# A hybrid encoder trunk on one core: each token block gets its own root, turn and split at the three norm borders

## The chip, the cores and the metric

One core of one Trainium2 chip. The metric is device time in microseconds of one launch; three runs of the kernel before took 2215.88, 2216.30 and 2216.88 us, median 2216.3.

## What is computed

x is 256 tokens by 2048 features, float32. Four sublayers follow, each `x = x + gate * mixer(norm(x) * gain + shift)`: a pooling mixer, a SwiGLU feed-forward (FFN), a gated linear recurrence (HGRN2), a second FFN. Then a last RMS norm.

```python
def rms_norm(x, gain):
    y = x * lax.rsqrt(jnp.mean(x * x, axis=-1, keepdims=True) + EPS)
    return y * gain

for layer in range(2):
    mod = silu(c) @ w_ada[layer] + b_ada[layer]
    sh_m, sc_m, g_m, sh_f, sc_f, g_f = split(mod, 6)
    h = rms_norm(x, norm_mix_gain[layer]) * (1 + sc_m) + sh_m
    y = pool_mixer(h, ...) if layer == 0 else hgrn2_mixer(h, ...)
    x = x + g_m * y
    h = rms_norm(x, norm_ffn_gain[layer]) * (1 + sc_f) + sh_f
    a, b = split(h @ w_ffn_in[layer], 2)
    x = x + g_f * ((silu(a) * b) @ w_ffn_out[layer])
return rms_norm(x, final_gain)
```

## The kernel before

**Tiling.** Tokens are two blocks of 128 (`TB` = 2), features are chunks of 512 (`CH`), each of four groups of 128. A product writes one chunk of 512 output columns for both token blocks into a PSUM tile `prod`. It runs over steps of 128 input features. To reach float32 accuracy with fp32r operands, each operand is split in a high and a low part, and each step is three matmuls per token block: hi x w_hi, hi x w_lo, lo x w_hi (lines 589 to 591), six per step. Weights come in pairs of steps: SyncE loads `raw`, ScalarE copies it to `w_hi` (line 907), VectorE subtracts to get `w_lo` (line 1232). There are four slots for pairs, so the pairs of the first four steps of the next product (`AHEAD` = 4) are made ready before a product ends, and the pair of step 4 is made after it.

**Who orders the work.** Everything is written out by hand. Each engine has its own program in its own order, with semaphores between them; within an engine's queue nothing passes anything. In a product, each engine calls small functions at given steps (`before(k)`, `after(k)`).

**A border** is the place where a residual x is complete and the next product needs norm(x). There are three: FFN 0 to recurrence (`FFN_OUT` to the first product `C_H`), recurrence's output product to FFN 1 (`C_A1`), and FFN 1 to the last norm. At each one:

1. The last four steps of the last product (`last_steps`, line 551) are done block by block: 12 matmuls of token block 0, then 12 of block 1.
2. VectorE (`update_last`, line 1414) multiplies each block by the gate (line 1427) and adds it to `xs` (line 1435). ScalarE (`square_last`, line 950) squares the last chunk of each block and sums it (line 959).
3. After both blocks, VectorE (`last_root`, line 1343) makes the variance of both and its reciprocal (lines 1346, 1349), and ScalarE the root `rstd` (line 977).
4. VectorE normalises a chunk of both blocks into `tok` (`normalise`, line 1367), TensorE turns it (eight 128x128 transposes, line 660; four fill the PSUM tile `small[0]`, four `small[1]`, each holding two feature groups of both blocks), ScalarE multiplies by the gain and adds the shift (`modulate`, line 989, four activations of 128x256), VectorE casts to `h_hi` (line 1371) and subtracts to `h_lo` (line 1374). All of chunk 0, and the turn of chunk 1, stand ahead of the first matmul of the next product. Chunk 1's modulate and split run beside steps 0 to 3.
5. The next product goes step by step, both token blocks in each. In the recurrence a further chunk is turned ahead of step 4 (k % HG == 0 in `features`); in FFN 1 none is.

After chunk 1's split VectorE makes `w_lo` of step 4. In FFN 1 it first does one "fold" (line 1278), a term of the next modulation vector (`w_ada`), which stands at step 2 in its order.

At the last border there is no turn: after the root of both blocks ScalarE scales block 0's first 1536 columns (line 1221) and block 1's first 512 (line 1222), VectorE the rest (lines 1837, 1842), and SyncE stores four pieces (lines 478 to 484).

Of the kernel before, what the change touches and what calls it, by code (L numbers as in the profile page):

```python
# [40 lines left out]
def build(nc, x, c, norm_mix_gain, norm_ffn_gain, w_ada, b_ada, pool_w, pool_scale, hgrn_w_in,  # L41
# [49 lines left out]
    LAST, BLOCKED = (C_OUT0 + NCH - 1, C_WOUT + NCH - 1, C_OUT1 + NCH - 1), 4  # L91
    FFN_IN = [HALF] * (4 * NA) + [KD] * (2 * (NF - NA))
# [71 lines left out]
    with ctx:  # L164
# [155 lines left out]
        block_modulated = sem("block_modulated")  # L320
        h_first = sem("h_first")
# [44 lines left out]
        def _(sp):  # L366
# [173 lines left out]
        def _(pe):  # L540
# [28 lines left out]

            def segment(chunk, hi, lo, first, n, after=None, before=None, begin=True, end=True):  # L570

                par = chunk % 2
                if begin and chunk >= 2:
                    evacuated(pe, chunk - 2)
                for s in range(n):
                    if chunk in LAST and s == n - BLOCKED:
                        last_steps(chunk, hi, lo, first + s)
                        break
                    if before is not None:
# [104 lines left out]
            def features(k):  # L684
                if k == 0:
                    turn_normalised()
# [60 lines left out]
            def ffn_in(layer):  # L747
                def first_half(s):
                    if s == 0 and layer:
                        turn_normalised()  # L750
                        turn_normalised()
                    wait_block(s)
# [145 lines left out]
        def _(act):  # L898
# [51 lines left out]
            def square_last(at):  # L950
                t.tick("upd")
                t.tick("last")
                for tb in range(TB):
                    if tb:
                        act.wait_ge(x_updated, t.get("upd"))
                    else:
                        act.wait_ge(block_updated, t.get("last"))
                    act.wait_ge(squared, t.get("sq"))
                    act.activation(junk[:, :], xs[:, tb, at * CH:(at + 1) * CH], ACT.Square,
                                   accum_out=ssq[:, tb, at:at + 1]).then_inc(squared, 1)  # L960
                    t.tick("sq")
# [48 lines left out]
            def features(k, gains, shifts, ready):  # L1010
                if k == 0:
                    act.wait_ge(gain_ready, ready)
                    modulate(gains, shifts, 0)
                    modulate(gains, shifts, 1)
                if k % HG == 0 and k // HG >= 2:
                    modulate(gains, shifts, k // HG)
# [53 lines left out]
            def ffn_in(layer):  # L1070
# [9 lines left out]
                def in_a(_):  # L1080
                    g = t.get("step")
                    if g == START[base_a]:
                        act.wait_ge(gain_ready, 7 if layer else 3)
                        act.wait_ge(unit_taken, UNIT[(layer, SH_F, 0) if layer else (0, MIX_F, 0)] + 1)
                        modulate(gain, shifts, 0)
                        if layer:
                            modulate(gain, shifts, 1)
# [33 lines left out]
            def ffn_out(layer):  # L1121
# [9 lines left out]
                sqrt_table()  # L1131
                square_last(NCH - 1)
                root()
# [60 lines left out]
            def first_features(k):  # L1194
                features(k, gain, mod[:, 0, 0:KD], 6)
# [17 lines left out]
            sqrt_table()  # L1213
            square_last(NCH - 1)
            root()

            ffn_in(1)
            ffn_out(1)
            act.wait_ge(x_gained, 2)
            act.wait_ge(rstd_ready, t.get("norm"))  # L1220
            act.activation(xs[:, 0, 0:D - CH], xs[:, 0, 0:D - CH], ACT.Copy, scale=rstd[:, 0:1]).then_inc(y_block, 1)
            act.activation(xs[:, 1, 0:CH], xs[:, 1, 0:CH], ACT.Copy, scale=rstd[:, 1:2]).then_inc(y_block, 1)

        @block.vector
        def _(dve):
# [117 lines left out]
            def last_root():  # L1343
                dve.wait_ge(early_ready, t.get("early"))
                dve.wait_ge(squared, t.get("sq"))
                dve.scalar_tensor_tensor(rstd[:, :], ssq[:, :, NCH - 1], 1.0 / D, early[:, :], ALU.mult, ALU.add).then_inc(var_step, 1)
                t.tick("var")
                dve.wait_ge(var_step, t.get("var"))
                dve.reciprocal(rstd[:, :], rstd[:, :]).then_inc(var_ready, 1)
                t.tick("norm")  # L1350
# [62 lines left out]

            def update_last(chunk_at, at, gates, unit):

                par = chunk_at % 2
# [4 lines left out]
                t.tick("last")  # L1421
                for tb in range(TB):
                    if tb:
                        multiplied(dve, chunk_at)
                    else:
                        dve.wait_ge(block_multiplied, t.get("last"))
                    gated = dve.tensor_tensor(tok[:, tb], prod[par][:, tb], gates, ALU.mult)
                    if tb:
                        gated.then_inc(prod_free[par], 1)
                        evacuated(dve, chunk_at)  # L1430
                    else:
                        gated.then_inc(block_gated, 1)
                        dve.wait_ge(block_gated, t.get("last"))
                    xc = xs[:, tb, at * CH:(at + 1) * CH]
                    added = dve.tensor_tensor(xc, xc, tok[:, tb], ALU.add)
                    if tb:
                        added.then_inc(x_updated, 1)
                    else:
                        added.then_inc(block_updated, 1)
                t.tick("sq", TB)  # L1440

# [123 lines left out]
            def ffn_in(layer):  # L1565
# [33 lines left out]
                def first_half(k):  # L1599
                    if k == 0:  # L1600
                        if layer:
                            normalise(0)
                            normalise(1, 1)
                        split_feat(0)
                        if layer:
                            split_feat(1)
# [50 lines left out]
            def ffn_out(layer):  # L1657
# [16 lines left out]
                last_root()  # L1674
# [156 lines left out]
            last_root()  # L1831
            ffn_in(1)
            ffn_out(1)
            dve.wait_ge(rstd_ready, t.get("norm"))
            for tb in range(TB):
# [27 lines left out]
```

## Time and profile before

| | |
|---|---|
| median of three runs | 2216.3 us |
| profiled execution, first to last instruction (span; no other time of it is recorded) | 2214.7 us |
| TensorE matmul busy | 2161.9 us, 98% of the span |
| VectorE busy | 1659.7 us, 75% |
| ScalarE busy | 998.5 us, 45% |
| mean granted TensorE clock | 0.989 |
| DMA | 574 MB, 259 GB/s |

A matmul's end is modelled, so busy TensorE isn't TensorE at its peak. The time in brackets in a timeline row is how long the engine was idle just before, and which instruction ended that. "Issue" there means that no releaser is seen.

### The profile page before, as it was taken

How to read it: one execution, taken by the hardware profiler on the slowest of the kernel's cores; microseconds unless marked ns; L12 is line 12 of the kernel's file. 1: busy time of each engine (PE TensorE's matmuls, PEld its weight loads, DVE VectorE, ACT ScalarE, POOL GpSimd, SP SyncE). 2: the span in 40 equal slices, each digit the busy share in tenths (PEclk: the TensorE clock that was granted, in tenths of full speed). 3: DMA queues.
4: the chain of work that ended last, by engine and by line, in shares of the span. 5: the costliest groups of instructions: out<-in, count | busy, mean ns of one | idle time of the engine just before them, and what ended most of it. 6: DMA issues, size and time to landing. Idle time of an engine off the chain costs nothing.

```text
span 2214.7 us, 25203 instructions
## 1 busy us (share of the span) xinstructions
PE 2161.9 (98%) x9785; PEld 1753.5 (79%) x9785; DVE 1659.7 (75%) x1709; ACT 998.5 (45%) x1116; POOL 17.9 (1%) x77
## 2 busy tenths in 40 slices
PE   7999999999999999999999999999999999999997
PEld 3547887888888888788888888878888888888886
DVE  5779899999988876578787888677755678456644
ACT  3224544444444444454645455544454444444343
POOL 1000000000000000100000000000000000000000
PEclk9999999999999999999999999999999999999999
DMA  9999998999899987476656664578866687658664
GB/s 374 407 399 350 330 336 305 320 321 317 312 343 312 325 296 239 148 237 202 216 171 206 203 200 136 181 248 301 301 183 190 190 265 258 181 190 290 242 214 138
DMA packets 250356, 574.38 MB, mean 259 GB/s; under 512 B 17558, under 2 KB 17750, under 8 KB 249724
## 3 DMA queue, kind: packets, MB, share of 16 engines
q1 hardware_dynamic: 250236, 572.77, 75.8%
q8 instruction: 77, 1.26, 0.2%
q14 instruction: 43, 0.35, 0.0%
HBM read 570.60 MB, written 2.10 MB: 259 GB/s over the span
## 4 chain that ended last, share of the span: by engine, by line
PE 91%; DVE 3%; SPq 2%; issue 2%; DMA 1%; ACT 1%; ACTq 0%; DVEq 0%
PE prod L589 27%; PE prod L591 27%; PE prod L590 27%; PE small L834 2%; PE modp L617 2%; DVE acc L1281 2%; PE small L660 1%; SPq L399 1%; DMA ada<-in_w_ada 1%; PE modp L651 1%; SPq L374 1%; PE small L806 0%; DMA ada_head<-in_w_ada 0%; PE modp L624 0%; DVE part_value L1577 0%
## 5 line engine op out<-in xcount | busy, mean ns | idle before, releaser
L907 ACT ACTIVATE w_hi<-raw 128x1024 fp32r<-128x1024 f32 x696 | 736.3, 1061 | 1025.4 <-PE prod L591 960.6
L1232 DVE TENSOR_TENSOR w_lo<-raw,w_hi 128x1024 fp32r<-128x1024 f32 x696 | 847.7, 1222 | 431.7 <-ACT w_hi L907 430.3
L589 PE MATMUL prod<-w_hi,h_hi 128*128 128x512 f32 x2072 | 821.4, 396 | 4.9 <-issue 1.9
L591 PE MATMUL prod<-w_hi,h_lo 128*128 128x512 f32 x2072 | 809.4, 391 | 0.0
L590 PE MATMUL prod<-w_lo,h_hi 128*128 128x512 f32 x2072 | 808.8, 390 | 0.0
L589 PEld LDWEIGHTS prod<-w_hi,h_hi 128*128 128x128 f32 x2072 | 390.9, 189 | 87.2 <-issue 3.4
L591 PEld LDWEIGHTS prod<-w_hi,h_lo 128*128 128x128 f32 x2072 | 390.4, 188 | 82.6
L590 PEld LDWEIGHTS prod<-w_lo,h_hi 128*128 128x128 f32 x2072 | 390.9, 189 | 79.7 <-issue 1.4
L1281 DVE SCALAR_TENSOR_TENSOR acc<-ada,cond,acc 128x1024 f32<-128x1024 f32 x255 | 325.8, 1278 | 0.4
L589 PE MATMUL prod<-w_hi,g_hi 128*128 128x512 f32 x688 | 268.8, 391 | 0.0
L591 PE MATMUL prod<-w_hi,g_lo 128*128 128x512 f32 x688 | 267.7, 389 | 0.0
L590 PE MATMUL prod<-w_lo,g_hi 128*128 128x512 f32 x688 | 267.7, 389 | 0.0
L589 PEld LDWEIGHTS prod<-w_hi,g_hi 128*128 128x128 f32 x688 | 129.2, 188 | 27.2 <-issue 0.5
L590 PEld LDWEIGHTS prod<-w_lo,g_hi 128*128 128x128 f32 x688 | 129.2, 188 | 27.1 <-issue 0.5
L591 PEld LDWEIGHTS prod<-w_hi,g_lo 128*128 128x128 f32 x688 | 129.2, 188 | 26.9
L617 PE MATMUL modp<-ada,cond_rows 128*128 128x512 f32 x112 | 58.3, 681 | 13.1 <-DMA brows<-in_b_ada 7.5
L617 PEld LDWEIGHTS modp<-ada,cond_rows 128*128 128x128 f32 x112 | 24.1, 221 | 43.9 <-issue 41.2
L834 PEld LDWEIGHTS small<-qdec,kdec 128*128 128x128 f32 (+1 forms) x448 | 50.6, 184 | 3.3 <-issue 1.4
L834 PE MATMUL small<-qdec,kdec 128*128 128x64 f32 (+1 forms) x448 | 50.0, 265 | 0.0
L660 PE MATMUL small<-ident,tok 128*128 128x128 f32 x272 | 37.8, 285 | 9.8 <-issue 7.9
L660 PEld LDWEIGHTS small<-ident,tok 128*128 128x128 f32 x272 | 33.2, 146 | 15.7 <-issue 9.2
L617 PE MATMUL modp<-ada_head,cond_rows 128*128 128x512 f32 x96 | 42.3, 592 | 0.0
(183 smaller groups left out, 1080.1 us busy)
## 6 DMA issues: line engine op xcount, KB each, us to landing
raw<-in_w_ffn_in SPq DMA_DIRECT2D x352, 512.0 KB, 4.8
ada<-in_w_ada SPq DMA_DIRECT2D x300, 512.0 KB, 6.1
raw<-in_w_ffn_out SPq DMA_DIRECT2D x176, 512.0 KB, 4.6
raw<-in_hgrn_w_in SPq DMA_DIRECT2D x128, 512.0 KB, 3.9
ada_head<-in_w_ada SPq DMA_DIRECT2D x84, 512.0 KB, 14.9
raw<-in_hgrn_w_out SPq DMA_DIRECT2D x32, 512.0 KB, 3.7
raw<-in_pool_w SPq DMA_DIRECT2D x8, 512.0 KB, 15.7
xs<-in_x SPq DMA_DIRECT2D x2, 1024.0 KB, 17.1
```

The source lines that it names most:

```text
L374: sp.dma_start(raw[:, slot], src.rearrange("(a p) n -> p a n", p=P)).then_inc(raw_loaded[slot], 16)
L399: sp.dma_start(ada_buffer(slot), block[:, at:at + UW]).then_inc(ada_loaded[slot], 16)
L589: pe.matmul(o, hi[:, k, ts], wh, start=(begin and s == 0), stop=False)
L590: pe.matmul(o, hi[:, k, ts], wl, start=False, stop=False)
L591: mm = pe.matmul(o, lo[:, k, ts], wh, start=False, stop=(end and s == n - 1))
L617: mm = pe.matmul(modp[:, o], cond_rows[:, k], ada_buffer(slot)[:, o * CH:(o + 1) * CH], start=(k == 0), stop=(in_columns(u) and k == n_row ...
L651: mm = pe.matmul(modp[:, o], ones[:, :], a[:, o * CH:(o + 1) * CH], start=not begun, stop=True)
L660: mm = pe.transpose(small[half][:, o:o + P], block_of(tb, 2 * half + j), ident[:, :])
L834: mm = pe.matmul(small[b][0:keys, o:o + H], kdec[:, b, hd, blk * P:blk * P + keys], qdec[:, b, hd, blk * H:(blk + 1) * H], start=True, sto ...
L907: act.activation(w_hi[:, slot], raw[:, r], ACT.Copy).then_inc(hi_ready, 1)
L1232: dve.tensor_tensor(w_lo[:, slot], raw[:, r], w_hi[:, slot], ALU.subtract).then_inc(lo_ready, 1)
L1281: ins = dve.scalar_tensor_tensor(a, ada_buffer(slot), cond[:, k:k + 1], a, ALU.mult, ALU.add)
```

## The change

The roots, turns and splits at a border are done per token block. `square_last` becomes `square_block`, `last_root` becomes `root_block`, `normalise(0)` becomes `normalise_block`. TensorE's first four steps of the next product are a function of their own (`first_steps`): block 0's turn, four steps of block 0 (with the turn of block 1 between steps 1 and 2), then four steps of block 1 (with the turn of chunk 1 ahead of its step 1). The first feature group of a block (the "column") is modulated and split alone, the other three together. At the last border block 0 is scaled as soon as its own root is there, and the order of the four stores changes.

```diff
@@ TensorE @@
+            def turn_block(tb):
+                pe.wait_ge(block_normalised, TB * t.get("border") + tb + 1)
+                bank(tb)
+                for b in range(HG):
+                    mm = pe.transpose(small[tb][:, b * P:(b + 1) * P], tok[:, tb, b * P:(b + 1) * P], ident[:, :])
+                filled(mm, tb)
+
+            def first_steps(chunk, hi, lo):
+                g = t.get("step")
+                pe.wait_ge(lo_ready, g // 2 + 1)
+                turn_block(0)
+                for tb in range(TB):
...
+                    for s in range(BLOCKED):
...
+                        if s == 0:
+                            pe.wait_ge(column_split, TB * t.get("border") + tb + 1)
+                        if s == 1:
+                            pe.wait_ge(block_split, TB * t.get("border") + tb + 1)
+                        if tb == 0 and s == 2:
+                            turn_block(1)
+                            pe.wait_ge(lo_ready, g // 2 + 2)
+                        if tb and s == 1:
+                            turn_normalised()
+                        pe.matmul(o, hi[:, s, ts], wh, start=(s == 0), stop=False)
+                        pe.matmul(o, hi[:, s, ts], wl, start=False, stop=False)
+                        mm = pe.matmul(o, lo[:, s, ts], wh, start=False, stop=False)
+                        if tb and s % 2:
+                            mm.then_inc(w_used, 1)
@@ ScalarE @@
+            def border(gains, shifts, ready, unit):
+                sqrt_table()
+                square_block(NCH - 1, 0)
+                root_block(0)
+                square_block(NCH - 1, 1)
+                act.wait_ge(gain_ready, ready)
+                act.wait_ge(unit_taken, unit + 1)
+                modulate_block(0, gains, shifts, [0])
+                root_block(1)
+                modulate_block(0, gains, shifts, list(range(1, HG)))
+                modulate_block(1, gains, shifts, list(range(HG)))
+                t.tick("border")
+                act.wait_ge(block_split, TB * t.get("border"))
+                modulate(gains, shifts, 1)
...
             ffn_out(1)
+            sqrt_table()
+            square_block(NCH - 1, 0)
+            root_block(0)
             act.wait_ge(x_gained, 2)
-            act.wait_ge(rstd_ready, t.get("norm"))
+            act.wait_ge(root_ready, TB * t.get("border") + 1)
             act.activation(xs[:, 0, 0:D - CH], ...)
+            square_block(NCH - 1, 1)
+            root_block(1)
+            act.wait_ge(root_ready, TB * t.get("border") + 2)
             act.activation(xs[:, 1, 0:CH], ...)
@@ VectorE @@
             def update_last(chunk_at, at, gates, unit):
...
+                update_block(chunk_at, at, gates, 0)
+                root_block(0)
+                update_block(chunk_at, at, gates, 1)
+            def split_block(tb):
...
+                for blocks, signal in ((slice(0, 1), column_split), (slice(1, HG), block_split)):
...
+                    dve.tensor_copy(h_hi[:, blocks, ts], both[:, blocks]).then_inc(h_high, 1)
...
+                    dve.tensor_tensor(h_lo[:, blocks, ts], both[:, blocks], h_hi[:, blocks, ts], ALU.subtract).then_inc(signal, 1)
+            def border():
+                normalise_block(0)
+                root_block(1)
+                t.tick("sq", TB)
+                split_block(0)
+                normalise_block(1)
+                dve.wait_ge(small_full[0], t.get("small0"))
+                normalise(1, 1)
+                split_block(1)
+                t.tick("border")
             def features(k):
                 if k == 0:
-                    normalise(0)
-                    for n in range(2):
-                        normalise(n + 1, 1)
-                        split_feat(n)
+                    normalise(2, 1)
+                    split_feat(1)
...
+            def scale_last(tb):
+                dve.wait_ge(root_ready, TB * t.get("border") + tb + 1)
...
+            scale_last(0)
+            root_block(1)
+            scale_last(1)
@@ SyncE @@
+            sp.wait_ge(y_block, 1)
+            sp.dma_start(out[0, 0:P, 0:last], xs[:, 0, 0:last]).then_inc(stored, 16)
             sp.wait_ge(y_ready, 1)
             sp.dma_start(out[0, 0:P, last:], xs[:, 0, last:]).then_inc(stored, 16)
-            sp.wait_ge(y_block, 1)
-            sp.dma_start(out[0, 0:P, 0:last], xs[:, 0, 0:last]).then_inc(stored, 16)
+            sp.wait_ge(y_block, 2)
+            sp.dma_start(out[0, P:S, 0:CH], xs[:, 1, 0:CH]).then_inc(stored, 16)
             sp.wait_ge(y_ready, 2)
             sp.dma_start(out[0, P:S, CH:], xs[:, 1, CH:]).then_inc(stored, 16)
-            sp.wait_ge(y_block, 2)
-            sp.dma_start(out[0, P:S, 0:CH], xs[:, 1, 0:CH]).then_inc(stored, 16)
```

## Rows read from the trace of the kernel before

**Rows 1.** The page's chain that ended last, shares of the span by engine
```profile
PE 91%; DVE 3%; SPq 2%; issue 2%; DMA 1%; ACT 1%; ACTq 0%; DVEq 0%
```

**Rows 2.** Timeline, first border: start us, us, engine, line, out<-in, count [idle before, releaser]
```profile
926.30 0.63 ACT L959 ACTIVATE junk<-xs 128x512 bf16<-128x512 f32 x1 [1.64 <-DVE xs L1435]
...
927.46 0.69 DVE L1427 TENSOR_TENSOR tok<-prod,gate 128x512 f32<-128x512 f32 x1 [1.20 <-PE prod L563]
...
929.74 0.16 DVE L1346 SCALAR_TENSOR_TENSOR rstd<-ssq,early 128x2 f32<-128x2 f32 x1 [0.86 <-ACT junk L959]
...
930.37 0.91 DVE L1367 TENSOR_SCALAR tok<-xs,rstd 128x512 f32<-128x512 f32 x2 [0.27 <-ACT rstd L977]
...
931.38 1.54 PE L660 MATMUL small<-ident,tok 128*128 128x128 f32 x8 [3.95 <-issue]
932.16 1.93 ACT L989 ACTIVATE feat<-small,mod,gain 128x256 f32<-128x256 f32 x4 [1.82 <-PE small L660]
...
935.52 0.78 PE L589 MATMUL prod<-w_hi,h_hi 128*128 128x512 f32 x1
...
939.47 2.35 DVE L1232 TENSOR_TENSOR w_lo<-raw,w_hi 128x1024 fp32r<-128x1024 f32 x2
...
942.52 1.03 PE L660 MATMUL small<-ident,tok 128*128 128x128 f32 x8
...
943.16 1.93 ACT L989 ACTIVATE feat<-small,mod,gain 128x256 f32<-128x256 f32 x4 [3.52 <-PE small L660]
...
943.31 0.48 PE L589 MATMUL prod<-w_hi,h_hi 128*128 128x512 f32 x1
...
943.59 0.88 DVE L1367 TENSOR_SCALAR tok<-xs,rstd 128x512 f32<-128x512 f32 x2 [1.78 <-PE small L660]
```

**Rows 3.** Timeline, second border
```profile
1459.62 0.69 DVE L1427 TENSOR_TENSOR tok<-prod,gate 128x512 f32<-128x512 f32 x1 [1.20 <-PE prod L563]
...
1470.25 0.75 DVE L1278 TENSOR_SCALAR acc<-ada,cond 128x1024 f32<-128x1024 f32 x1
...
1470.91 1.22 DVE L1232 TENSOR_TENSOR w_lo<-raw,w_hi 128x1024 fp32r<-128x1024 f32 x1
...
1474.64 0.39 PE L589 MATMUL prod<-w_hi,h_hi 128*128 128x512 f32 x1
```

**Rows 4.** Windows, first border: length, busy (count) by engine, clock, DMA share, GB/s
```profile
931.38:935.52 4.14, 3.16 (x16) 2.76 (x17) 2.49 (x7) 2.04 (x5) 4.07 (x11) 0.55 0.00 0
935.52:938.65 3.13, 3.13 (x9) 2.46 (x8) 3.06 (x7) 2.84 (x6) 0.89 (x2) 0.50 0.00 0
```

**Rows 5.** Groups by form, whole kernel: busy us, mean ns of one, idle before
```profile
L989 ACT ACTIVATE feat<-small,mod,gain 128x256 f32<-128x256 f32 x48 | 23.4, 563 | 29.4 <-PE small L660 26.7 <-DVE h_lo L1374 2.4 <-DVE gain L1355 0.2
...
L1029 ACT ACTIVATE cond_rows<-ones,zero,cond 128x128 f32<-128x128 f32 x9 | 3.6, 477 | 0.0
...
L1374 DVE TENSOR_TENSOR h_lo<-feat,h_hi 128x512 fp32r<-128x512 f32 x29 | 20.1, 693 | 1.0
...
L1371 DVE CAST h_hi<-feat 128x512 fp32r<-128x512 f32 x29 | 12.4, 429 | 1.8 <-ACT feat L989 1.7
...
L1374 DVE TENSOR_TENSOR h_lo<-feat,h_hi 128x256 fp32r<-128x256 f32 x6 | 2.5, 424 | 0.2
...
L1371 DVE CAST h_hi<-feat 128x256 fp32r<-128x256 f32 x6 | 1.9, 313 | 0.6 <-ACT feat L989 0.6
```

**Rows 6.** Timeline, end of the kernel
```profile
2206.60 1.57 ACT L1221 ACTIVATE xs<-xs,rstd 128x1536 f32<-128x1536 f32 x1
2207.32 0.36 SPq L478 DMA_DIRECT2D out<-xs  x1
...
2209.09 0.94 SPq L484 DMA_DIRECT2D out<-xs  x1
```

**Rows 7.** Windows, end of the kernel, columns as in rows 4
```profile
2208.00:2209.00 1.00, 0.00 (x0) 0.00 (x0) 0.62 (x1) 0.79 (x2) 0.00 (x0) 0.70 0.68 262
...
2210.00:2211.00 1.00, 0.00 (x0) 0.00 (x0) 0.00 (x0) 0.00 (x0) 0.00 (x0) 0.50 0.99 399
```

More of the change, by code:

```diff
@@ L578, in segment @@
                         break
+                    if chunk in FIRST and s < BLOCKED:
+                        if s == 0:
+                            first_steps(chunk, hi, lo)
+                        continue
                     if before is not None:
@@ L948, in square, with square_block @@
                     t.tick("sq")
[L950 to L961, printed above, removed]
+            def square_block(at, tb):
+                if tb:
+                    t.tick("upd")
+                    act.wait_ge(x_updated, t.get("upd"))
+                else:
+                    act.wait_ge(block_updated, t.get("border") + 1)
+                act.wait_ge(squared, t.get("sq"))
+                act.activation(junk[:, :], xs[:, tb, at * CH:(at + 1) * CH], ACT.Square,
+                               accum_out=ssq[:, tb, at:at + 1]).then_inc(squared, 1)
+                t.tick("sq")
@@ new lines, in root_block, with modulate_block @@
+            def root_block(tb):
+                act.wait_ge(root_var, TB * t.get("border") + tb + 1)
+                act.activation(rstd[:, tb:tb + 1], rstd[:, tb:tb + 1], ACT.Sqrt).then_inc(root_ready, 1)
+            def modulate_block(tb, gains, shifts, blocks):
+                if blocks[0] == 0:
+                    filled(tb)
+                    act.wait_ge(h_ready, t.get("h"))
+                for b in blocks:
+                    ins = act.activation(feat[:, b // 2, b % 2, tb * P:(tb + 1) * P], small[tb][:, b * P:(b + 1) * P], ACT.Identity,
+                                         bias=shifts[:, b:b + 1], scale=gains[:, b:b + 1])
+                    if b == 0:
+                        ins.then_inc(column_modulated, 1)
+                    if b == HG - 1:
+                        ins.then_inc(small_free[tb], 1)
@@ L1008, in pooled, with features @@
                     t.tick("h")
[L1010 to L1014, printed above, removed]
+            def features(k, gains, shifts):
                 if k % HG == 0 and k // HG >= 2:
@@ L1130, in ffn_out @@
                     ahead()
-                sqrt_table()
-                square_last(NCH - 1)
-                root()
+                    border(gain, mod[:, 0, 0:KD], 6, UNIT[(1, SH_M, 1)])
             ffn_out(0)
@@ L1194, in first_features @@
             def first_features(k):
-                features(k, gain, mod[:, 0, 0:KD], 6)
+                features(k, gain, mod[:, 0, 0:KD])
                 recurrence(k)
@@ L1341, in early_squares, with root_block @@
                 dve.tensor_scalar(early[:, :], early[:, :], 1.0 / D, EPS, ALU.mult, ALU.add).then_inc(early_ready, 1)
-            def last_root():
+            def root_block(tb):
+                n = TB * t.get("border") + tb
                 dve.wait_ge(early_ready, t.get("early"))
[L1345 to L1350, printed above, removed]
+                dve.wait_ge(squared, t.get("sq") + tb + 1)
+                dve.scalar_tensor_tensor(rstd[:, tb:tb + 1], ssq[:, tb, NCH - 1:NCH], 1.0 / D, early[:, tb:tb + 1],
+                                         ALU.mult, ALU.add).then_inc(last_var, 1)
+                dve.wait_ge(last_var, n + 1)
+                dve.reciprocal(rstd[:, tb:tb + 1], rstd[:, tb:tb + 1]).then_inc(root_var, 1)
             def gains_of(gains, branch, first, n, unit):
@@ L1412, in update, with update_block @@
                 t.tick("sq", TB)
+            def update_block(chunk_at, at, gates, tb):
+                par = chunk_at % 2
+                if tb:
+                    multiplied(dve, chunk_at)
+                else:
+                    dve.wait_ge(block_multiplied, t.get("border") + 1)
+                gated = dve.tensor_tensor(tok[:, tb], prod[par][:, tb], gates, ALU.mult)
+                if tb:
+                    gated.then_inc(prod_free[par], 1)
+                    evacuated(dve, chunk_at)
+                else:
+                    gated.then_inc(block_gated, 1)
+                    dve.wait_ge(block_gated, t.get("border") + 1)
+                xc = xs[:, tb, at * CH:(at + 1) * CH]
+                added = dve.tensor_tensor(xc, xc, tok[:, tb], ALU.add)
+                added.then_inc(x_updated if tb else block_updated, 1)
             def update_last(chunk_at, at, gates, unit):
-                par = chunk_at % 2
                 early_squares()
@@ L1440, in update_last, with normalise_block @@
-                t.tick("sq", TB)
+            def normalise_block(tb):
+                dve.wait_ge(root_ready, TB * t.get("border") + tb + 1)
+                if tb:
+                    dve.wait_ge(x_updated, t.get("upd"))
+                else:
+                    dve.wait_ge(block_updated, t.get("border") + 1)
+                dve.tensor_scalar(tok[:, tb], xs[:, tb, 0:CH], rstd[:, tb:tb + 1], None, ALU.mult).then_inc(block_normalised, 1)
+            def split_block(tb):
+                n, ts = TB * t.get("border") + tb, slice(tb * P, (tb + 1) * P)
+                t.tick(f"small{tb}")
+                both = feat[:, :, :, ts].rearrange("p a b s -> p (a b) s")
+                for blocks, signal in ((slice(0, 1), column_split), (slice(1, HG), block_split)):
+                    if blocks.start:
+                        dve.wait_ge(small_free[tb], t.get(f"small{tb}"))
+                    else:
+                        dve.wait_ge(column_modulated, n + 1)
+                    dve.tensor_copy(h_hi[:, blocks, ts], both[:, blocks]).then_inc(h_high, 1)
+                    t.tick("hh")
+                    dve.wait_ge(h_high, t.get("hh"))
+                    dve.tensor_tensor(h_lo[:, blocks, ts], both[:, blocks], h_hi[:, blocks, ts], ALU.subtract).then_inc(signal, 1)
@@ L1673, in ffn_out @@
                 update_last(base + NCH - 1, NCH - 1, gate[:, 1], UNIT[(layer, G_F, 1)])
-                last_root()
+                if layer == 0:
+                    border()
             ffn_out(0)
@@ L1830, in _ @@
             update_last(C_WOUT + NCH - 1, NCH - 1, gate[:, 1], UNIT[(1, G_M, 1)])
-            last_root()
+            border()
             ffn_in(1)
             ffn_out(1)
-            dve.wait_ge(rstd_ready, t.get("norm"))
-            for tb in range(TB):
+            def scale_last(tb):
+                dve.wait_ge(root_ready, TB * t.get("border") + tb + 1)
                 xc = xs[:, tb, D - CH:]
```

56 lines of the change are left out of this document (19 added, 37 removed).

## The prediction

> **What bounds the kernel now.** I read the chain that ended last first: TensorE holds 91% of it [rows 1]. A change pays only where TensorE stands still, so I went to the timeline around the three places where a residual finishes and the norm of the whole row has to be known. I count from the moment T at which VectorE begins to gate the second token block, 927.46 at the first border (FFN to recurrence), 1459.62 at the second (recurrence to FFN) [rows 2, 3].
>
> At the first border the reader should follow one chain [rows 2]: gate and add to 928.9 (VectorE then waits 0.86 for ScalarE's square), variance 929.74, root, normalise 930.37, turn 931.38 (TensorE idle 3.95 us before it), modulate 932.16, a second round of eight turns, and the first matmul of the next product at 935.52, T+8.06. Its first four steps are 24 matmuls; step 4 begins at 943.31, T+15.85. From there on TensorE runs without a gap, so **the place to compare is the start of step 4**: what comes before it counts only as far as it moves that. At the second border step 4 begins at 1474.64, T+15.02 (no turn stands ahead of it there) [rows 3]. w_lo for step 4 begins at 939.47 and 1470.91, well ahead of use in both [rows 2, 3].
>
> The clock matters too. TensorE's granted clock is 0.55 of full (between 1.2 and 2.4 GHz) over 931.38 to 935.52 and 0.50 (1.2 GHz) over 935.52 to 938.65 [rows 4]. Those 3.13 us bring the first matmul to the eighth, 0.43 to 0.45 us each; the 16 that follow until the turn at 942.52 take 0.23 each. Before that the engine had been idle for 3.95 us and had then done transposes with gaps.
>
> At the end of the kernel a 1.58 us scale on ScalarE starts at 2206.60, the first store is issued at 2207.32, the last at 2209.09 [rows 6]; bytes move from a little after 2208.2 at 0.4 MB per us [rows 7], so 2.10 MB of output take 5.25 us, and end near 2213.5.
>
> **The change, part by part (clock at 2.4 GHz first).**
>
> *Own root for block 0.* One 0.16 variance and a reciprocal of 0.17 go between the square of block 0 (from 926.30, done 0.73 later, 927.03) and the gating of block 1. They end near 927.48: the gate starts 0.04 late. Bounds 0 to 0.1 us. Add ends 928.92, normalise of block 0 (one half of the 0.91 at 930.37, so 0.48) ends 929.32.
>
> *Turn of block 0.* Four transposes, 929.42. ScalarE started 0.78 after the first of four in the old order (931.38 to 932.16), so 930.20.
>
> *First column.* The trace has no 128x128 modulate from PSUM; the bounds are the 128x256 one, 0.56, and 128x128 from SBUF, 0.48 [rows 5]. I take 0.46, since the slope from the larger forms is about 0.1 us per 128 elements. Cast and subtract 128x128: from 0.43/0.31 and 0.69/0.42 for 512/256 elements [rows 5], 0.23 and 0.29. First matmul 931.34, **4.2 us earlier than before**.
>
> *The rest of block 0.* ScalarE: root of block 1 (0.2), three blocks at 0.35 from start to start (four of 256 elements take 1.93, so 0.46 apart, less 0.1 for 128 elements), done 931.96. VectorE casts 384 elements, 0.37, subtracts 0.56, done 932.95. TensorE: step 1 at 933.02, turn of block 1 at 933.70, 0.13 each as at 942.52 (eight in 1.03), so 934.22; steps 2 and 3 to 935.58.
>
> *Block 1.* VectorE cannot start the next chunk's normalise before that turn: 934.35, 0.8. Then column (ready 935.69) and three blocks (ScalarE 935.86, VectorE 936.85). Step 0 of block 1 goes at 935.77; before step 1 stands the turn of the next 512 features, at 936.92 = T+9.46. TensorE has 0.47 us in hand there.
>
> *What is late next.* In the old order that turn had run ahead of the first matmul; now it comes at T+9.46 and VectorE's queue is strictly behind it. First border: the next normalise starts 1.07 after a turn's start (942.52 to 943.59), takes 0.80, two casts and two subtracts take 2.24 end to end [rows 5], I take 2.12 since each starts a little before the last ends, w_lo 1.22: done 942.13, so step 4 at 942.20, **1.1 us earlier**. TensorE itself would have been ready at 936.92+1.03+9x0.227+1.03 = 941.0; it waits 1.2 us. Second border: no normalise, but ScalarE finishes the second half 0.64+1.93 = 2.57 after the turn's start (942.52, 943.16), then come half of the 2.12, the fold that stands ahead of w_lo (0.66 from 1470.25 to 1470.91), 1.22: T+15.05 against T+15.02, **0.0**. TensorE would have been ready at T+12.5. Fresh work on VectorE and ScalarE (two more modulates of overhead, two more cast and subtract pairs) is in these sums. After step 4 the queues have several us in hand in both traces: nothing more moves. The loads that SyncE issues behind w_lo go out up to 1.5 us later, against an idle of 1.5 us or more ahead of each later pair: 0.
>
> *The clock.* The chain above holds 3 matmuls of step 1, four transposes, six matmuls of steps 2 and 3 and three of step 0. At 1.2 GHz throughout, they cost 0.6+0.3+1.2+0.3 more, less the 0.47 in hand: the turn comes 1.9 later, and everything behind it. Border 1 is then 0.8 later than before, border 2 1.9 later. I weigh the two ends by the nearest rows: 4.0 us idle with a few transposes at its end was followed by the low clock. The new stretch from T to T+5.56 has 0.5 us of transposes and 0.7 us of matmuls in it, so it is nearer to the old one than to a busy stretch. But the work from T+5.56 on is dense, so the clock should be back sooner than in the old order. I take half of the 1.9: border 1 -0.15, border 2 +0.95.
>
> The Trainium skill (TensorE: Matmul & The Clock Gate, HAM oscillation) advises to keep idle gaps short so that the clock isn't taken back. It speaks for the change: the gap of 3.95 becomes gaps of 2.0, 1.5 and up to 0.9. By it the clock stays at 2.4 GHz; that is rival 1 below. The low clock behind 3.95 us of idle agrees with it; gaps as short as the new ones with so little between them no row shows.
>
> *The end.* The scale at 2206.60 stands 2.97 behind T, as the normalise at 930.37 stood 2.91 behind it, so T is 2203.63. Block 0's variance is done by then, its root 2203.88, ScalarE scales 1536 columns to 2205.54. That stands ahead of block 1's square: it waits 0.4 beyond its input (T+1.45 becomes T+1.83). Behind it the root at 2206.9, then VectorE's scales of 512 and 1024 columns, 0.75 each like half of ScalarE's 1.58, to 2208.33. Stores: first at 2205.6 instead of 2207.32, last at 2208.4 instead of 2209.09. The order of stores only follows this. If bytes run continuously from 1.7 us earlier, the end moves by 1.7. Bounds: 0.7 (the last issue alone) and 1.8. I take **1.6**, since the last 0.79 MB, at 0.4 per us and behind the third store, end near 2211.8.
>
> **Sum.** -0.15 + 0.95 - 1.6 = -0.8 us. Profiled span 2214.7, so 2213.9; the median lies 1.6 above that span, and I add it: **2215.5**.
>
> **Rivals.**
> 1. *The clock stays at 2.4 GHz* in both borders: -1.1 + 0.0 - 1.6 = -2.7, 2213.6. For: shorter gaps; against: 1.2 us of work in 5.6 us.
> 2. *Slower: the restart is paid at 1.2 GHz and by VectorE's queue.* The later turn holds back w_lo of step 4. From a turn at T+10.6 on border 1 loses, from T+9.4 on border 2 does. With the low clock until the turn: +0.8+1.9-1.6 = +1.1, 2217.4; without the full gain at the end +2.0, 2218.3. For: old rows; against: dense work from T+5.56.
> 3. *VectorE's queue doesn't hold step 4*, only TensorE's chain does: -2.3 - 2.5 - 1.6 = -6.4, 2209.9. For: the first matmul is 4 us earlier. Against: in program order w_lo stands behind the splits, as at 939.47.
> 4. *The change does nothing at the end*: the square held by the long scale eats the gain, stores end as before; 2217.
>
> **Chances.** Forecast 0.50, rival 1 0.20, rival 2 0.17, rival 3 0.07, rival 4 0.06. A difference of 0.2%, 4.4 us, is about what a measurement of this kernel can tell from no change; only rival 3 reaches it on the fast side, and nothing but an error of mine on the slow side. Faster 0.09, same 0.88, slower 0.03. The range takes in rivals 1 and 2's first price with some margin for the 128x128 costs: 2212.6 to 2217.9.
>
> **What would show it.** Right: first matmul of the next product near T+3.9; a wait of TensorE for w_lo (VectorE) ahead of step 4 of 1 to 3 us at both borders, longer at the second; step 4 at T+14.7 to T+16.7 and T+15 to T+17; the clock at 1.2 GHz somewhere between T+4 and T+11; the first store near 2205.6 less what was won before. Wrong: no wait for w_lo at step 4, or a step 4 before T+14 at either border, or an end unchanged from the last matmul on (11.1 us before).

## The result and the profile after

The changed kernel takes 2219.8 us (median of 14 runs, 2217.4 to 2222.2), the kernel before 2216.3 (14 runs, 2214.3 to 2218.3). The ratio is 1.0017, 95% interval 1.0009 to 1.0024: slower by 0.17%, clear of noise. The prediction said 2215.5 and 2212.6 to 2217.9, a little faster. It was wrong in sign.

The profiled execution of the changed kernel has these first lines (span; the chain that ended last, by engine). VectorE's share of the chain rose from 3% to 4% [rows 1].

```profile
span 2217.5 us, 25230 instructions
...
PE 90%; DVE 4%; SPq 2%; issue 2%; DMA 1%; ACT 1%; DVEq 0%; ACTq 0%
```

The waits of TensorE at the first border (928 to 1010) and at the second (1456 to 1560): engine, line, what it waited for, us in total, times, longest.

```profile
PE small L583 <- DVE tok L1517: 3.7, 1, 3.7
PE prod L606 <- DVE h_lo L1532: 1.7, 1, 1.7
PE prod L637 <- DVE w_lo L1301: 1.4, 1, 1.4
```

```profile
PE prod L637 <- DVE w_lo L1301: 2.8, 1, 2.8
PE small L583 <- DVE tok L1517: 2.1, 1, 2.1
PE prod L606 <- DVE h_lo L1532: 1.3, 1, 1.3
```

Two things stand out. The first turn waits 3.7 us for VectorE's normalise at one border and 2.1 at the other. And the step whose weights aren't ready (L637 is the first matmul of step 4) waits at both.

The timeline of the first border answers to [rows 2]. A row of GpSimd is in it, an engine that the prediction doesn't mention.

```profile
926.93 0.69 DVE L1489 TENSOR_TENSOR tok<-prod,gate 128x512 f32<-128x512 f32 x1
...
928.26 1.81 POOL L533 MEMSET kdec<- 128x2048 f32 x1
928.27 2.07 DVE L1517 TENSOR_SCALAR tok<-xs,rstd 128x512 f32<-128x512 f32 x1
...
930.60 0.63 PE L583 MATMUL small<-ident,tok 128*128 128x128 f32 x4 [3.71 <-DVE tok L1517]
...
931.89 0.60 DVE L1529 CAST h_hi<-feat 128x128 fp32r<-128x128 f32 x1 [1.25 <-ACT feat L1013]
...
939.36 1.10 PE L708 MATMUL small<-ident,tok 128*128 128x128 f32 x8
...
943.42 2.35 DVE L1301 TENSOR_TENSOR w_lo<-raw,w_hi 128x1024 fp32r<-128x1024 f32 x2
...
944.78 0.47 PE L637 MATMUL prod<-w_hi,h_hi 128*128 128x512 f32 x1 [1.37 <-DVE w_lo L1301]
```

The normalise of one block, 0.48 us of work, lasts 2.07: it started 0.01 us behind a 1.81 us memset of GpSimd and ended 0.27 after it. Step 4 stands at T+17.85, where it was at T+15.85 [rows 2].

The kernel before already had these memsets, and a sign that GpSimd can hold VectorE: a cast beside GpSimd's selects took 0.67 at the first border, the same cast 0.42 at the second, where GpSimd did nothing. Four rows of that kernel:

```profile
928.79 1.80 POOL L525 MEMSET kdec<- 128x2048 f32 x1
...
933.22 3.19 POOL L536 TENSOR_SCALAR_AFFINE_SELECT masks<-masks 128x64 f32<-128x64 f32 x7
...
935.24 0.67 DVE L1371 CAST h_hi<-feat 128x512 fp32r<-128x512 f32 x1
...
1466.88 0.42 DVE L1371 CAST h_hi<-feat 128x512 fp32r<-128x512 f32 x1
```

The second border, which answers to [rows 3]. Normalise is 0.48 here, and GpSimd does nothing. The first matmul of the next product is at T+3.97, in the kernel before at T+7.70 (1467.32).

```profile
1461.08 0.69 DVE L1489 TENSOR_TENSOR tok<-prod,gate 128x512 f32<-128x512 f32 x1
...
1462.41 0.48 DVE L1517 TENSOR_SCALAR tok<-xs,rstd 128x512 f32<-128x512 f32 x1
...
1465.05 0.79 PE L606 MATMUL prod<-w_hi,h_hi 128*128 128x512 f32 x1 [1.27 <-DVE h_lo L1532]
...
1471.80 1.09 PE L708 MATMUL small<-ident,tok 128*128 128x128 f32 x8
...
1475.74 0.75 DVE L1347 TENSOR_SCALAR acc<-ada,cond 128x1024 f32<-128x1024 f32 x1
1476.40 1.22 DVE L1301 TENSOR_TENSOR w_lo<-raw,w_hi 128x1024 fp32r<-128x1024 f32 x1
...
1477.76 0.77 PE L637 MATMUL prod<-w_hi,h_hi 128*128 128x512 f32 x1 [2.78 <-DVE w_lo L1301]
```

The last row's 0.77 (against 0.39 for such a matmul at 2.4 GHz [rows 3]) shows that the clock fell a second time. Windows behind it, columns as in [rows 4]:

```profile
1475.00:1477.00 2.00, 0.00 (x0) 0.00 (x0) 1.97 (x4) 2.00 (x3) 0.00 (x0) 1.00 0.00 0
1477.00:1478.00 1.00, 0.24 (x1) 0.27 (x2) 1.00 (x2) 1.00 (x2) 0.00 (x0) 0.72 0.00 0
1478.00:1480.00 2.00, 2.00 (x5) 1.56 (x6) 2.00 (x3) 0.26 (x1) 0.00 (x0) 0.50 0.63 145
```

TensorE stood idle for 2.78 us, the clock fell to 1.2 GHz at its end, and seven matmuls ran at 0.43 us each instead of 0.23: 1.4 us, lost after the point that I had called the end of the border.

The end of the kernel, which answers to [rows 6]; T is 2208.30 there.

```profile
2208.65 1.58 ACT L1287 ACTIVATE xs<-xs,rstd 128x1536 f32<-128x1536 f32 x1
...
2210.25 0.36 SPq L486 DMA_DIRECT2D out<-xs  x1
...
2213.02 0.33 SPq L492 DMA_DIRECT2D out<-xs  x1
```

From T to the last instruction it is 9.20 us, before 11.07 (2214.7 - 2203.63).

**The balance, in one execution each** (span +2.8): until T of the first border -0.5 (nothing is changed there; the 13 profiled executions put T at 926.1 to 929.0), first border +2.0, between the borders 0.0, second border +1.7, from its step 4 to the last T +1.55 (728.99 became 730.54), the end -1.9.

This table has the same readings from each run's timeline, for the experiments below: the medians are of all runs of a kernel, the other columns of its one profiled execution. The kernel before, measured again beside them, had 2216.2 (e1 to e4), 2215.8 (e5 to e8) and 2216.3 (e9 to e11). "Rest" is from step 4 of the second border to the last T; "tail" from there to the last instruction.

| kernel | median us | step 4, border 1 | step 4, border 2 | rest | tail |
|---|---|---|---|---|---|
| before | 2216.3 | T+15.85 | T+15.02 | 728.99 | 11.07 |
| after | 2219.8 | 17.85 | 16.68 | 730.54 | 9.20 |
| e1_pool_late | 2218.0 | 16.36 | 16.77 | 730.69 | 9.24 |
| e2_wlo_early | 2214.8 | 16.22 | 13.50 | 730.72 | 9.21 |
| e3_end_only | 2214.2 | 15.37 | 14.95 | 729.03 | 9.24 |
| e4_pool_wlo | 2213.3 | 14.43 | 13.75 | 730.75 | 9.21 |
| e5_wlo_two | 2211.8 | 14.55 | 13.59 | 729.14 | 9.25 |
| e6_wlo_two_busy | 2211.1 | 14.06 | 13.26 | 729.15 | 9.13 |
| e7_old_order_busy | 2209.1 | 13.36 | 12.65 | 729.00 | 9.13 |
| e8_sweep | 2221.1 (1 run) | 16.00 | 18.34 | 730.59 | 9.20 |
| e9_wlo_one_busy | 2210.7 | 13.25 | 12.46 | 730.72 | 9.17 |
| e10_old_busy_only | 2211.7 | 13.64 | 12.65 | 729.02 | 11.05 |
| e11_new_busy_only | 2216.7 | 16.47 | 15.41 | 729.12 | 9.20 |

Where two kernels have the same code at the first border, step 4 still differs by 0.4 to 0.5 us (e3 and before, e8 and e1). The clock was low for stretches of different length there: about 3.4 us in e8 and 6.8 in e1, as windows of 1 us show.

### The profile page after: what moved, and what is told of

Its sections match the earlier page's. It is cut to its first block, busy times and chain, and to the rows that moved or that the text cites. A ratio compares the mean times of both kernels' runs of the same rounds, so it can differ in the third digit from the quotient of the medians.

```text
span 2217.5 us, 25230 instructions
## 1 busy us (share of the span) xinstructions
PE 2164.4 (98%) x9785; PEld 1753.2 (79%) x9785; DVE 1663.7 (75%) x1719; ACT 1000.7 (45%) x1127; POOL 17.3 (1%) x77
## 4 chain that ended last, share of the span: by engine, by line
PE 90%; DVE 4%; SPq 2%; issue 2%; DMA 1%; ACT 1%; DVEq 0%; ACTq 0%
PE prod L637 27%; PE prod L639 27%; PE prod L638 27%; PE small L877 2%; PE modp L665 2%; DVE acc L1350 2%; SPq L407 1%; PE small L708 1%; DMA ada<-in_w_ada 1%; PE modp L699 1%; SPq L382 1%; PE small L849 0%; DMA ada_head<-in_w_ada 0%; DVE w_lo L1301 0%; DVE part_value L1681 0%
## 5 line engine op out<-in xcount | busy, mean ns | idle before, releaser
L637 PE MATMUL prod<-w_hi,h_hi 128*128 128x512 f32 x2056 | 814.3, 396 | 9.1 <-DVE w_lo L1301 4.2
L637 PEld LDWEIGHTS prod<-w_hi,h_hi 128*128 128x128 f32 x2056 | 387.2, 188 | 91.3 <-issue 8.2
L637 PE MATMUL prod<-w_hi,g_hi 128*128 128x512 f32 x688 | 268.9, 391 | 0.0
L637 PEld LDWEIGHTS prod<-w_hi,g_hi 128*128 128x128 f32 x688 | 129.1, 188 | 27.2 <-issue 0.5
L1350 DVE SCALAR_TENSOR_TENSOR acc<-ada_head,cond,acc 128x1024 f32<-128x1024 f32 x29 | 37.2, 1284 | 3.5 <-DMA ada_head<-in_w_ada 1.2
L665 PEld LDWEIGHTS modp<-ada_head,cond_rows 128*128 128x128 f32 x96 | 18.2, 190 | 23.0 <-issue 23.0
```

Of the source, the lines that this page charges most:

```text
L665: mm = pe.matmul(modp[:, o], cond_rows[:, k], ada_buffer(slot)[:, o * CH:(o + 1) * CH], start=(k == 0), stop=(in_columns(u) and k == n_row ...
L1350: ins = dve.scalar_tensor_tensor(a, ada_buffer(slot), cond[:, k:k + 1], a, ALU.mult, ALU.add)
```

## The experiments

**GpSimd's constants, moved away (e1) and moved in (e8).** GpSimd waits for the recurrence's first product instead of the product ahead of it:

```diff
-            multiplied(pool, C_H - 1)
+            multiplied(pool, C_H)
```

> The changed kernel with one edit: GpSimd makes the recurrence's constants (memsets of 0.95, 0.47 and 1.81 us, then 14 selects) after the first product of the recurrence instead of at the first border. Theory A (GpSimd's memset holds VectorE's normalise, 2.07 us there against 0.48 at the second border): the normalise at the first border takes 0.48, the cast of 128x128 0.23 instead of 0.60, step 4 of the first border comes at T+15.8 to T+16.3 instead of T+17.85, and the time falls by 1.5 to 2 us against the changed kernel, to 2217.6 to 2218.3. Rival (the 2.07 is a wait for a semaphore or for memory traffic of another kind, GpSimd has nothing to do with it): normalise stays near 2 us, no change of time.

2218.0 us (11 runs, 2215.5 to 2219.5; ratio to before 1.0007, 0.9998 to 1.0016). The memsets now run at 961 to 964, and the normalise and first cast of the first border are:

```profile
928.45 0.48 DVE L1517 TENSOR_SCALAR tok<-xs,rstd 128x512 f32<-128x512 f32 x1
...
930.47 0.23 DVE L1529 CAST h_hi<-feat 128x128 fp32r<-128x128 f32 x1 [0.73 <-ACT feat L1013]
```

Theory A holds: step 4 at T+16.36 instead of 17.85, 1.5 us. The other run puts the same work where it had done no harm:

```diff
+            multiplied(pool, C_A1 - 1)
+            for first, end in ((0, 4), (4, 6), (8, 16)):
+                pool.memset(g_hi[:, first:end, :].bitcast(F32), 0.0).then_inc(swept, 1)
```

> The kernel e1_pool_late with three memsets of GpSimd put at the second border (1024, 512 and 2048 elements of an unused part of g_hi), as its constants stood at the first one in the changed kernel. If GpSimd's memset holds VectorE's normalise, the 0.48 us normalise at T+1.35 of the second border takes about 2.0 us, until the third memset ends, and the first cast behind it 0.4 to 0.6 instead of 0.23, while gate, add and variance (tensor-tensor forms) keep their 0.69 and 0.16. If it was something of the first border (its data, its loads), normalise stays at 0.48.

Timeline of the second border, VectorE and then GpSimd:

```profile
1461.27 0.69 DVE L1498 TENSOR_TENSOR tok<-prod,gate 128x512 f32<-128x512 f32 x1
1462.00 0.69 DVE L1506 TENSOR_TENSOR xs<-xs,tok 128x512 f32<-128x512 f32 x1
1462.61 2.13 DVE L1526 TENSOR_SCALAR tok<-xs,rstd 128x512 f32<-128x512 f32 x1
...
1466.28 0.23 DVE L1538 CAST h_hi<-feat 128x128 fp32r<-128x128 f32 x1 [1.29 <-ACT feat L1018]
```

```profile
1461.30 3.16 POOL L550 MEMSET g_hi<- 128x1024 f32 x3 [490.09 <-PE prod L576]
```

Normalise lasts 2.13 until the memsets are over, while the tensor-tensor gate and add beside the same memsets keep 0.69. Step 4 of this border is 1.6 us later than in e1 (T+18.34 against T+16.77). The slower cast that I expected didn't come (0.23): no GpSimd work was left by then, where in the changed kernel the masks' selects ran beside it. That the memset holds the normalise is shown from both sides.

**w_lo of step 4 made inside the border (e2, e4, e5).**

```diff
+                for _ in range(EARLY):
+                    hi()
...
+                for _ in range(EARLY):
+                    lo()
```

The first two lines are ScalarE's, ahead of its modulate of block 1, the others VectorE's, ahead of `normalise(1, 1)`. `EARLY` is 1 here, in e4 and in e9, and 2 in e5 and e6.

> The changed kernel with one edit: ScalarE's and VectorE's halves of the weight pair of step 4 are made inside the border, in VectorE's idle stretch of 2.2 us ahead of the second block's turn, not behind the split of the next chunk. Theory B (the restart is held by VectorE's queue: TensorE waits 1.4 and 2.8 us for w_lo at step 4, and the 2.8 us of idle drop the clock a second time, 7 matmuls at 0.43 instead of 0.23): both waits are gone or under 0.3 us, no second drop of the clock behind 1477, step 4 at the second border near T+13.9 instead of T+16.7, time lower by 1.2+2.8+1.4 = 5 us, near 2214.5, under the kernel before. Rival (what is late next is the split h_lo or TensorE's own chain, just behind): waits move to h_lo, under 1.5 us gained.

2214.8 us (2213.7 to 2216.3; ratio 0.9993, 0.9984 to 1.0001): 5.0 below the changed kernel, as expected. TensorE has no wait for w_lo at step 4 of either border, and step 4 of the second is at T+13.50, 3.2 earlier. A part of the wait moved on, to step 6:

```profile
1478.73 0.47 PE L637 MATMUL prod<-w_hi,h_hi 128*128 128x512 f32 x1 [1.35 <-DVE w_lo L1303]
```

Its 0.47 tells that the clock didn't fall behind this shorter wait. So "rest" stays long (730.72), now for the wait and not for the clock. The rival (w_lo isn't what holds) falls.

> The changed kernel with both edits: GpSimd's constants later, and the weight pair of step 4 inside the border. If the two causes are the whole of the loss and add up, step 4 stands at T+14.9 at the first border and T+13.9 at the second (before: 15.85 and 15.02), and the time is near 2212.5, 7 us below the changed kernel and 4 below the one before. If per-block order itself is bad (more instructions on ScalarE and VectorE, longer chain), it stays at or above 2214.4, what the end alone gives.

2213.3 us (2211.7 to 2215.8; ratio 0.9988, 0.9979 to 0.9997). Step 4 came 0.5 and 0.15 earlier than expected (14.43, 13.75), but the wait at step 6 (1.36), which I had not put in, keeps the time 0.8 above. It is the first version in the new order whose interval lies below the kernel before. It is 0.9 us below what the end alone gives (e3), less than these runs can tell from nothing, as each kernel's runs spread over 3 to 4 us.

> As the run with both edits (GpSimd's constants later, weight pair of step 4 inside the border), with the pair of step 6 inside the border as well. In that run TensorE still waited 1.4 us for w_lo at step 6 of the second border, where a fold of VectorE stands ahead. Theory: that wait goes, 744.5 us from the second border's T to the last one's T become 743, time near 2212.0. Rival: two subtractions (2.3 us) overrun VectorE's idle stretch of 2.2 us and push the second block's chain back, no gain.

2211.8 us (2210.7 to 2214.5; ratio 0.9983, 0.9974 to 0.9992). The wait at step 6 is gone and "rest" is back at 729.14. The rival's overrun can't be seen yet: TensorE's steps at the low clock make VectorE's idle stretch longer, as e6 will show.

**The end alone (e3).** `square_block`, `root_block` and the new order of stores put into the kernel before, at the last border only (the indented lines now run for the first FFN alone).

```diff
-                sqrt_table()
-                square_last(NCH - 1)
-                root()
+                    sqrt_table()
+                    square_last(NCH - 1)
+                    root()
...
+            sqrt_table()
+            square_block(NCH - 1, 0)
+            root_block(0)
...
+            square_block(NCH - 1, 1)
+            root_block(1)
```

> The kernel before with the last border of the change alone (own root for each block, scale of block 0 ahead of the square of block 1, stores in the new order). Theory: the tail from the gate of block 1 to the last instruction is 9.2 us as in the changed kernel, instead of 11.07: time 2214.4, 1.9 below before. Rival (the end's gain in the changed kernel came from a chance of the transfers): the tail stays above 10.5, time unchanged.

2214.2 us (2213.0 to 2216.4; ratio 0.9993, 0.9983 to 1.0002), tail 9.24. The median fell by 2.0, the tail by 1.8; the interval of the ratio just takes in 1, so the 1.8 rests on the tails, which are 9.13 to 9.25 in all eleven kernels with the new end and 11.05 and 11.07 in the two without. The first two borders cost 2219.8 - 2214.2 = 5.6 by the medians, 5.2 by the balance.

**The clock (e6, e7, e9, e10, e11).** Idle matmuls read a ready weight pair, write a free PSUM tile and do nothing else:

```diff
+            def keep_busy(n, unit):
+                pe.wait_ge(unit_taken, unit + 1)
+                slot = t.get("step") // 2 % SPL
+                pe.wait_ge(lo_ready, t.get("step") // 2 + 1)
+                for _ in range(n):
+                    pe.matmul(modp[:, 0], w_hi[:, slot, 0, 0:P], w_hi[:, slot, 0], start=True, stop=True)
```

> As e5_wlo_two, with 8 idle matmuls ahead of block 0's turn and 5 behind it, which read the ready weight pair and write a free PSUM tile: they only keep TensorE at work in the 2.1 and 1.3 us of waiting. Theory C (the low clock in the restart costs 1.2 us a border: the next chunk's turn comes at T+10.7 where the chain at 2.4 GHz, worked out before, gives T+9.5): granted clock stays 1.0 through both borders, turn at T+9.4 to T+9.7, step 4 at T+12.5 to T+13.5, time 2.4 us lower, near 2209.6. Rival: the clock falls all the same, or the added matmuls hold back the turns they stand ahead of; turn at T+10.7 or later, time the same or longer.

2211.1 us (2210.1 to 2213.3; ratio 0.9979, 0.9970 to 0.9988). The clock is 1.00 over both borders, windows as in [rows 4]:

```profile
926.50:932.00 5.50, 4.92 (x22) 3.19 (x20) 3.68 (x11) 3.35 (x9) 0.00 (x0) 1.00 0.08 31
932.00:937.00 5.00, 3.59 (x16) 2.49 (x16) 4.93 (x10) 2.58 (x6) 0.00 (x0) 1.00 0.38 110
```

but it brought 0.7 instead of 2.4, too little to tell from nothing by the medians: the next chunk's turn came at T+10.26. With TensorE faster, VectorE's idle stretch is shorter, and now the two subtractions do overrun it (2.35 us from 932.54, the next normalise at 934.81, the turn it waits for full by 933.72).

> As e6_wlo_two_busy (per-block order, GpSimd's constants later, idle matmuls) with only the pair of step 4 made early. There, at the full clock, the two subtractions of 2.35 us overran VectorE's idle stretch and the next chunk's turn came at T+10.26. Theory: with one pair the turn comes at T+9.5 as the prediction's chain at 2.4 GHz said, step 4 at T+13.3 and T+12.6; at the second border 1 us of waiting for w_lo comes back at step 6. Time 2210.4 to 2211.0, still above e7_old_order_busy (2209.1). Rival: the turn stays at T+10 or later (something other than w_lo holds it).

2210.7 us (2209.0 to 2212.8; ratio 0.9977, 0.9968 to 0.9986). The turn is at T+9.45 and T+9.46, step 4 at T+13.25 and T+12.46, all as expected; the 1.3 us for w_lo at step 6 of the second border is back. So `w_lo` and the border's own chain share one short queue, and either of these two orders costs about a microsecond: 1.1 us of waiting for h_lo in e6, 1.3 for w_lo here. The medians (2211.1, 2210.7) don't tell them apart. The fold that stands ahead of w_lo was left in its place in every run; whether moving it would free the queue stays open.

> The kernel before (both blocks through one root, one turn and one split at the first two borders) with the last border of the change, GpSimd's constants later, and idle matmuls: 16 ahead of the first turn, 3 between the two turns. Theory: the clock stays at 2.4 GHz there too; step 4 comes 1.6 to 2.4 us earlier than T+15.85 and T+15.02, that is T+13.7 and T+12.9: time near 2210.2. If that is no more than e6_wlo_two_busy shows, the per-block order with all its mending buys nothing over the old order with a warm clock. Rival: per-block order is worth 1 us a border by itself, and this kernel stays 1.5 us or more above e6_wlo_two_busy.

2209.1 us (6 runs, 2207.6 to 2210.0; ratio 0.9969, 0.9958 to 0.9981), the fastest of all, 6.7 below the kernel before measured beside it (2215.8). First matmul and step 4 of the next product at the two borders:

```profile
933.42 0.47 PE L599 MATMUL prod<-w_hi,h_hi 128*128 128x512 f32 x1
...
939.78 0.48 PE L599 MATMUL prod<-w_hi,h_hi 128*128 128x512 f32 x1
...
1463.20 0.47 PE L599 MATMUL prod<-w_hi,h_hi 128*128 128x512 f32 x1
...
1468.77 0.39 PE L599 MATMUL prod<-w_hi,h_hi 128*128 128x512 f32 x1
```

The first matmul is at T+7.0, 3.2 us behind that of e9 (T+3.8), and step 4 is at the same place (13.36 and 12.65 against 13.25 and 12.46). After it TensorE has no wait, where e9 has the 1.3 at step 6, so that its "rest" is 1.7 longer. The start that the per-block order wins is given back before step 4.

> The kernel before with the idle matmuls alone (16 ahead of the first turn, 3 behind it, at the first two borders). If the low clock alone made T+15.85 and T+15.02, step 4 comes at T+13.5 and T+12.7 and the time is 4 to 4.7 us below before, 2211.5. If GpSimd's constants and the end had the larger share of e7_old_order_busy's gain of 6.7, it stays above 2213.

2211.7 us (2210.2 to 2213.3; ratio 0.9980, 0.9971 to 0.9988): the low clock cost the kernel before 4.5 us, 2.2 and 2.4 at the borders.

> The changed kernel with the idle matmuls alone (8 ahead of block 0's turn, 5 behind it). The clock's share there: first border T+17.85 to about T+16 (GpSimd still holds the normalise), second border T+16.7 to T+15.1, and, if TensorE's 2.8 us wait for w_lo isn't followed by the low clock this time, another 1.4: time 2215.5 to 2217. If the clock hardly matters in the changed order since VectorE sets the pace anyway, step 4 moves by less than 0.5 and the time stays above 2218.5.

2216.7 us (2215.4 to 2217.5; ratio 1.0001, 0.9992 to 1.0010), 3.1 below the changed kernel. At the second border the turn and step 4:

```profile
1471.13 1.09 PE L718 MATMUL small<-ident,tok 128*128 128x128 f32 x8 [0.17 <-DVE h_lo L1542]
...
1477.08 0.47 PE L647 MATMUL prod<-w_hi,h_hi 128*128 128x512 f32 x1 [2.79 <-DVE w_lo L1311]
```

T is 1461.67, so the turn is at T+9.46 and step 4 at T+15.41. The wait for w_lo is the same 2.79, and this time the clock stays (0.47, and "rest" 729.12). The same idle stretch was followed by the low clock in the profiled executions of the changed kernel, e1 and e8, and not here. What decides it isn't shown; the clock had been low a few us before it in those three, and here it had not.

## Why the prediction was wrong, point by point

- *Where to look, and who is late next.* Right. TensorE waits at step 4 for w_lo at both borders (1.4 and 2.8 against "1 to 3, longer at the second"), and the first matmul came early at the second border (T+3.97, 3.9 foretold). At the first it came at T+5.99, and step 4 at T+17.85, outside the T+14.7 to T+16.7 that were named for it; at the second, T+16.68, inside. Rival 3, which let VectorE's queue off, fell.
- *The chain at 2.4 GHz.* Right where the clock holds and GpSimd is out of the way (both borders of e9, the second of e11): the next chunk's turn is at T+9.45 and T+9.46, foretold T+9.46. From there to step 4 it measures 5.42 and 5.95 (e11), foretold 5.28 and 5.59; the two terms were 0.1 and 0.4 short.
- *The normalise of block 0, "so 0.48", which "ends 929.32".* **This step failed.** It was taken from VectorE's own rows, for a place at which it hadn't stood before. Moving it 1.6 us earlier put it beside GpSimd's memset: 2.07 us, and step 4 of the first border 1.5 later than without (e1; e8 shows the same hold elsewhere). In the kernel before the same memset ended at 930.59, 0.22 after the normalise began, and the row of two normalises shows 0.91 against 0.88 elsewhere [rows 2]. The prediction checked the queues of TensorE, ScalarE, VectorE and the loads, and not GpSimd's.
- *The clock, "I take half of the 1.9".* Mis-sized. In e1 the turn came at T+10.99 and T+10.87, in the changed kernel T+10.72 at the second border: 1.3 to 1.5 of the possible 1.9; in e8's first border it was 1.1 (T+10.57). The reason given for rival 1, shorter gaps, didn't hold: at the second border the clock fell behind 2.11 us of idle and four transposes.
- *After step 4 "nothing more moves".* **This failed too.** The 2.8 us wait that the prediction itself foresaw at the second border was followed by a second stretch at 1.2 GHz: 1.4 us of the 1.55 in "rest". It had the rows to suspect it: [rows 4] show a low clock behind an idle stretch of 3.95 us; I applied them to the gap that was there and not to the one that the change made.
- *The end.* Right in the mechanism: tail -1.87, foretold -1.6, just past the upper of the bounds 0.7 and 1.8; -1.83 in e3. Rival 4 fell.
- Sum by these steps: forecast -0.8; plus 1.5 (GpSimd), 1.6 (behind step 4, 1.4 of it the second fall), 0.5 and 0.3 (clock in each border), 0.1 and 0.4 (chain), less 0.3 (end) gives +3.3, where the medians differ by 3.5 and the profiled spans by 2.8 (0.5 of it from before the first border). Rival 2 had the right mechanism for the sign, with 1.1 to 2.0 as its price; both failed steps were missing in it. The range allowed for errors of durations, not for one more mechanism. The prediction also took 4.4 us as the least that a measurement could tell; 14 runs of each kernel told 3.5 apart, with an interval of less than 0.1% on either side.

Would the clock staying up have been enough, as rival 1 said? No: e11 is level with the kernel before (1.0001), since w_lo and GpSimd remain. In the forms tried, the order as such gains nothing once the clock holds: e9 and e7, both with GpSimd out of the way, put step 4 at the same place, and e9 then waits once more.

## What to carry to other kernels

An instruction that is moved keeps its work, not its duration: read what every engine does at its new place, GpSimd's idle-looking constants included. Before a dependent chain is cut into finer pieces, follow the queue of the slower engine up to the next step that needs it; 3.7 us won at the first matmul of the second border were worth nothing at the fifth step. Where TensorE must wait for a norm, price the low clock that follows: some twenty matmuls into a free tile at each border, which compute nothing, brought 4.5 us in the kernel before (e10), about as much as all the reordering without them at its best (e5, 4.1 below the kernel before measured beside it).

## What the runs showed of the hardware

- A 128x512 float32 tensor-scalar of VectorE (SBUF to SBUF) was held while GpSimd wrote by memset: 2.07 and 2.13 us against 0.48, ending 0.27 and 0.28 after the memset. That is less than its own 0.48, so some of it was done or overlapped before; no run shows how. Gate and add (two inputs) beside such memsets took their 0.69, and in e1 a 128x1024 subtraction its 1.23. Casts beside GpSimd's selects were slower too: 0.60 against 0.23 for 128x128, 0.67 against 0.42 for 128x512. The Trainium skill has this (SBUF — State Buffer, Who interferes with whom): copies, casts and tensor-scalars may use a port pair that VectorE shares with GpSimd, held by one of the two for a whole instruction, and tensor-tensor forms only clash with GpSimd's reads. The traces agree for the tensor-scalar, the casts and the memsets; beside the selects, which read, a 128x128 subtraction took 0.34 instead of 0.29.
- The clock fell to 1.2 GHz behind 3.95 and 3.93 us of idle at the two borders of the kernel before, during the turn that followed. At the second border of the changed kernel it fell behind 2.11 us of idle and four transposes, and again behind 2.78; the latter in three profiled executions of four. With 8 and 5 matmuls at the two places (new order), or 16 and 3 (old order), it stayed at 2.4 GHz at both borders in the profiled executions of all five kernels that had them.
